# Experts in a fixed loop of 16 with four kinds of work, in place of a computed list of items

## The chip, the cores and the metric

The kernel runs on one core of one Trainium2 chip. The metric is device time in microseconds (us) of one execution; lower is better. A core has a matrix engine (TensorE, PE), a vector engine (VectorE, DVE), an activation engine (ScalarE, ACT), GpSimd (POOL) and SyncE (SP), which here only issues transfers. Each engine runs a program of its own and meets the others through semaphores.

## The reference, cut to what matters

Two layers, each a hybrid attention block and a mixture of experts, on 256 tokens of 1024 numbers, all in fp32. What the change touches is the second half of a layer:

```python
def grouped_moe(h, w_router, b_router, w_gate, w_up, w_down):
    probs = jax.nn.softmax(xt @ w_router + b_router)      # 256 tokens x 16 experts
    # 4 groups of 4 experts: the best group, then the best 2 experts inside it
    experts, gates = ...                                  # 512 (token, expert) pairs in all
    for each expert e, for the tokens that chose it:
        a = silu(x @ w_gate[e]) * (x @ w_up[e])           # 1024 x 1024 each
        out += gate * (a @ w_down[e])                     # 1024 x 1024
h = layer_norm(ALPHA * h + out)
```

Every expert's three matrices (4 MB each, 12.6 MB together) are read from HBM once in a layer, 16 experts, two layers.

## The kernel before, in words

**Staging of the weights.** `ring` is an SBUF buffer of 16 slots of 1 MB. Slots 0 to 3 (EVEN) and 12 to 15 (ODD) take the gate matrices of even and odd experts, 4 to 7 (UP) the up matrix, 8 to 11 (DOWN) the down matrix. SP issues the transfers in a fixed order (`load_matrix`, L335 to L344), two slots at a time, each after the semaphores `ring_free` of its slots. TensorE adds to `ring_free` when it has used a slot. So the weights run at most about an expert and a third ahead of TensorE.

**The list of items.** After the router, DVE counts the tokens of each expert (`count`, at most 256) and makes a list of at most 19 items (L1271 to L1305). An expert with more than 128 tokens has two items, each other expert one. For each item the list holds the expert's number (`expert_i`), a kind (`kind_i`) and whether it is the expert's last item (`last_i`); `n_i` is the number of items, and `start_i` the items of the layers before, from which every engine computes the values that it waits for. The kind is 0 (tiny, up to 32 tokens), 1 (narrow, up to 64), 2 or 3 (wide, the first or second 128 tokens).

**The loop over the items.** PE, ACT and DVE each run a loop over `n` items with a branch for each kind. In the PE's program (L856 to L890): read `expert_i`, `kind_i`, `odd_i` (and `last_i` where the item isn't tiny) from SBUF into registers (`value_load`), wait for `xg_ready` (the gathered tokens), then branch. For tiny items gate and up products run side by side (`tiny_gate_up`, L566); for narrow ones gate, then up (`narrow_gate`, `narrow_item`, L554); for wide ones likewise (`wide_gate`, `wide_item`, L670), and the wide code stands there twice: once for an expert's last item, which frees the ring's slots, once for one that is not. Then each item gathers the tokens of the next (L541), turns the activations, multiplies by the down matrix, and scatters into `acc` (L622, L729). ACT computes silu (L1008, L1014, L1020), DVE the product with up (L1324, L1333, L1342) and the 0/1 matrices that pick tokens (`place_tokens`, `place_gates`).

In the profiled execution each layer has 16 items, none of them a second half. With t for tiny, n for narrow and w for wide, in their order:

```
layer 0:  t n n n n n t t t t t n t t t t
layer 1:  w w t w t t n t t t t t t t t t
```

Of the kernel before, what the change touches and what calls it, by code (L numbers as in the profile page):

```python
# [52 lines left out]
MOST = NEXP + (2 * SEQ - 1) // (P + 1)  # L53
ITEMS = MOST + 1
# [23 lines left out]
C_L16 = C_LO + 8 * 16  # L78
C_ODD = C_L16 + NEXP * NEXP
# [3 lines left out]
def constants():  # L83
# [31 lines left out]
    t[:, C_L16:C_L16 + 256] = (e[None] <= e[:, None]).astype(np.float32).ravel()  # L115
# [44 lines left out]
def build(nc, x, w_in, w_out, w_gate, w_up, w_down, small, router, ln, consts, out):  # L160
    with ExitStack() as ctx:
# [42 lines left out]
        rank_tab = sb("rank_tab", [P, TB, NEXP])  # L204
        gate_tab = sb("gate_tab", [P, TB, NEXP])
        nsub = sb("nsub", [P, 2, NEXP])
        wide_shift = sb("wide_shift", [P, 1])
        wide = sb("wide", [P, NEXP + 1])
        kind_step = sb("kind_step", [P, 2, NEXP])
        itab = sb("itab", [P, 4, ITEMS])  # L210
        startf = sb("startf", [P, DEPTH + 1])

        start_i = sb("start_i", [P, DEPTH + 1], I32)
        n_i = sb("n_i", [P, DEPTH], I32)
        expert_i = sb("expert_i", [P, DEPTH * ITEMS], I32)
        kind_i = sb("kind_i", [P, DEPTH * ITEMS], I32)
        odd_i = sb("odd_i", [P, NEXP], I32)
        last_i = sb("last_i", [P, DEPTH * ITEMS], I32)
# [80 lines left out]
        plan_ready = sem("plan_ready")  # L299
        dve_step = sem("dve_step")  # L300

        place_ready, gathered, xg_ready = sem("place_ready"), sem("gathered"), sem("xg_ready")
# [97 lines left out]
        def _(pe):  # L400
# [135 lines left out]
            def gather(ks, release=None):  # L536


                for k in ks:
# [6 lines left out]
                    if k % 4 == 3:  # L546
                        mm.then_inc(gathered, 1)
# [10 lines left out]
            def turn_gates():  # L558
# [3 lines left out]
                mm.then_inc(placeT_done, 1)  # L562
# [6 lines left out]
            def tiny_gate_up(first, gate_full, full):  # L569


                for i in range(4):
# [13 lines left out]
                    else:  # L586
                        gate.then_inc(gate_done, 1)
                        up0.then_inc(ring_free[first + 3], 1)
                        up1.then_inc(up_done, 1)

            def tiny_item(full, g, turn):

                pe.wait_ge(place_ready, turn + 1)
                gather(range(3), ring_free[UP + 3])
                pe.wait_ge(act_ready, g + 1)
                turn_gates()
                for b in range(4):
                    mm = nc.tensor.transpose(lo[:, 1, b * W:(b + 1) * W], act[0:W, b * P:(b + 1) * P], ident[0:W, 0:W])
                mm.then_inc(act_turned, 1)
                gather(range(3, 4))  # L600
                pe.wait_ge(act_t_ready, g + 1)
                for s in range(4):
# [8 lines left out]
                    mm.then_inc(down_done if s == 3 else ring_free[DOWN + s], 1)  # L611
                pe.wait_ge(placeT_ready, g + 1)
                gather(range(4, KB), ring_free[DOWN + 3])
                scatter_halves(g)

            def scatter_halves(g):

                pe.wait_ge(y_ready, g + 1)
# [5 lines left out]
                mm.then_inc(scattered, 1)  # L624

            def narrow_gate(first, gate_full, full):

                for i in range(4):
# [5 lines left out]
                    mm.then_inc(gate_done if i == 3 else ring_free[first + i], 1)  # L634
# [3 lines left out]
            def narrow_item(full, g, turn):  # L638

                for i in range(4):  # L640
# [4 lines left out]
                    mm.then_inc(up_done if i == 3 else ring_free[UP + i], 1)  # L645
                pe.wait_ge(place_ready, turn + 1)
                gather(range(3), ring_free[UP + 3])
                pe.wait_ge(act_ready, g + 1)
                for b in range(4):
                    mm = nc.tensor.transpose(lo[:, 1, b * P:(b + 1) * P], act[:, b * P:(b + 1) * P], ident)  # L650
                mm.then_inc(act_turned, 1)
                turn_gates()
                gather(range(3, 4))
                pe.wait_ge(act_t_ready, g + 1)
# [19 lines left out]
            def wide_gate(last, first, gate_full, full):  # L674

                for i in range(4):
# [5 lines left out]
                    if i == 3:  # L682
                        mm.then_inc(gate_done, 1)
                    elif last:
                        mm.then_inc(ring_free[first + i], 1)
# [689 lines left out]
```

## Time and profile before

| what | value |
|---|---|
| median of 3 runs | 1367.46 us (1367.44 to 1370.69) |
| the profiled execution's own time | 1370.7 us |
| its span, first to last instruction | 1369.0 us |
| mean granted TensorE clock | 0.908 |
| busy: PE, DVE, ACT | 1122.7, 312.4, 182.1 us |
| DMA | 444.83 MB, mean 325 GB/s |
| chain that ended last | PE 61%, DMA 29%, issue 6%, DVE 3% |

How to read it: the span is cut into 40 slices of 34.2 us, and a row of GB/s gives what DMA moved in each. Where this stands at about 429, DMA is full. "issue" in the chain is time in which an engine waited for nothing that the profile shows. The engines' own control instructions (register, branch, value loads) are not counted as busy, but the view of a source line lists them with their durations, under names such as PEldq and DVEq.

### The profile page before, as it was taken

The numbers are of one execution on the slowest core, as the hardware profiler recorded it, in microseconds if no ns is written. First come the engines' busy times: TensorE is split into PE (matmuls) and PEld (weight loads), VectorE is DVE, ScalarE is ACT, GpSimd is POOL, SyncE is SP. The second block draws the span as 40 slices with busy tenths as digits, with TensorE's granted clock in tenths as the row PEclk, the third lists the DMA queues.
The fourth block names the chain that finished last, engine by engine and source line by source line (L and its number), as shares of the span: only waits on it lengthen the run. The fifth ranks groups of instructions, "written<-read, shape, count | busy, mean of one in ns | idle before, by whom it ended". The sixth has DMA issues, their size and how long they took to land.

```text
span 1369.0 us, 17057 instructions
## 1 busy us (share of the span) xinstructions
PE 1122.7 (82%) x6068; PEld 571.9 (42%) x6069; DVE 312.4 (23%) x791; ACT 182.1 (13%) x373; POOL 4.6 (0%) x12
## 2 busy tenths in 40 slices
PE   7999877799977768679799975999998876577775
PEld 5776443344433233224577644445443332222232
DVE  0443531111111111112254443001111111111113
ACT  2233210001000100001223320100000100000100
POOL 0000000000000000000000000000000000000000
PEclk9999878899988899789899986999999998778888
DMA  9814319899999999999931430656989999999994
GB/s 367 360 62 164 143 44 426 350 419 428 429 428 428 429 428 429 429 428 423 419 135 62 185 143 13 246 199 264 383 326 374 429 429 428 428 428 428 428 429 204
DMA packets 34712, 444.83 MB, mean 325 GB/s; under 512 B 4080, under 2 KB 4336, under 8 KB 5872
## 3 DMA queue, kind: packets, MB, share of 16 engines
q1 hardware_dynamic: 33520, 440.08, 77.6%
q0 software_dynamic: 1152, 4.19, 0.8%
q8 instruction: 27, 0.44, 0.1%
q14 instruction: 13, 0.11, 0.0%
HBM read 443.22 MB, written 1.05 MB: 325 GB/s over the span
## 4 chain that ended last, share of the span: by engine, by line
PE 61%; DMA 29%; issue 6%; DVE 3%; SPq 1%; ACT 0%; DVEq 0%; ACTq 0%
DMA ring<-in_w_up_dram 23%; PE lo L566 13%; PE lo L670 9%; PE lo L554 9%; PE acc L453 8%; DMA ring<-in_w_down_dram 6%; PE acc L431 5%; PE lo L541 3%; PE acc L529 3%; PE acc L622 1%; PE lo L836 1%; PE acc L505 1%; PE lo L493 1%; PE acc L729 1%; PE lo L529 1%
## 5 line engine op out<-in xcount | busy, mean ns | idle before, releaser
L566 PE MATMUL lo<-ring,work 128*32 128x512 f32 x2112 | 276.0, 671 | 150.7 <-DMA ring<-in_w_up_dram 131.4
L566 PEld LDWEIGHTS lo<-ring,work 128*32 128x32 f32 x2112 | 68.2, 121 | 339.0 <-issue 164.0
L554 PE MATMUL lo<-ring,work 128*64 128x512 f32 x672 | 153.0, 611 | 26.4 <-issue 23.5
L541 PEld LDWEIGHTS lo<-work,h 128*128 128x128 f32 x1088 | 130.2, 193 | 53.8 <-issue 49.7
L541 PE MATMUL lo<-work,h 128*128 128x128 f32 x1088 | 146.6, 285 | 2.5 <-DVE work L1266 2.5
L670 PE MATMUL lo<-ring,work 128*128 128x512 f32 x288 | 126.8, 601 | 15.8 <-issue 15.8
L453 PE MATMUL acc<-actT,ring 128*128 128x256 f32 x512 | 119.2, 388 | 0.0
L453 PEld LDWEIGHTS acc<-actT,ring 128*128 128x128 f32 x512 | 98.6, 195 | 14.7 <-issue 1.6
L554 PEld LDWEIGHTS lo<-ring,work 128*64 128x64 f32 x672 | 48.3, 140 | 125.9 <-issue 116.6
L670 PEld LDWEIGHTS lo<-ring,work 128*128 128x128 f32 x288 | 55.2, 193 | 84.7 <-issue 84.7
L1324 DVE TENSOR_TENSOR work<-lo,work 64x512 f32<-64x512 f32 x22 | 15.0, 682 | 291.8 <-ACT work L1008 291.8
L1008 ACT ACTIVATE work<-lo 64x512 f32<-64x512 f32 x22 | 13.1, 593 | 492.2 <-PE lo L566 492.2
L431 PE MATMUL acc<-ring,actT 128*128 128x512 f32 x128 | 63.3, 640 | 4.0 <-ACT actT L909 4.0
L622 PE MATMUL acc<-work 64*128 64x512 f32 x232 | 57.6, 615 | 0.0
L1145 DVE COPY work<-lo 128x512 f32<-128x512 f32 x64 | 44.3, 692 | 56.9 <-PE lo L541 56.8
L529 PE MATMUL acc<-ring,work 128*128 128x512 f32 x104 | 48.9, 602 | 0.0
L431 PEld LDWEIGHTS acc<-ring,actT 128*128 128x128 f32 x128 | 25.1, 204 | 32.1 <-issue 30.7
L406 PE MATMUL lo<-cst,h 128*128 128x128 f32 x64 | 12.8, 365 | 25.9 <-DVE h L1053 18.2
L1329 DVE COPY work<-lo 128x512 f32<-128x512 f32 x22 | 15.2, 692 | 78.9 <-PE lo L566 78.9
L1333 DVE TENSOR_TENSOR work<-lo,work 128x512 f32<-128x512 f32 x7 | 4.8, 692 | 115.3 <-PE lo L554 115.3
L1138 DVE TENSOR_SCALAR work<-cst,rank_tab,gate_tab 128x128 f32 x64 | 19.3, 344 | 51.9 <-issue 51.9
L1008 ACT ACT_TABLE_LOAD x22 | 28.2, 1283 | 18.6 <-issue 18.5
(183 smaller groups left out, 691.8 us busy)
## 6 DMA issues: line engine op xcount, KB each, us to landing
ring<-in_w_gate_dram SPq DMA_DIRECT2D x64, 2048.0 KB, 12.9
ring<-in_w_up_dram SPq DMA_DIRECT2D x64, 2048.0 KB, 18.7
ring<-in_w_down_dram SPq DMA_DIRECT2D x64, 2048.0 KB, 24.1
ring<-in_w_in_dram SPq DMA_DIRECT2D x24, 1024.0 KB, 25.0
ring<-in_w_out_dram SPq DMA_DIRECT2D x8, 1024.0 KB, 29.5
ln_gb<-in_ln_dram POOLq DMA_DIRECT2D x8, 512.0 KB, 7.0
cst<-in_consts_dram SPq DMA_DIRECT2D x1, 1544.0 KB, 17.9
h<-in_x_dram SPq DMA_DIRECT2D x1, 1024.0 KB, 5.2
```

Of the source, the lines that this page charges most:

```text
L431: mm = nc.tensor.matmul(acc[:, 3 if u else 1, :], actT[:, k, t * P:(t + 1) * P], ring[:, s, (k % 4) * CH:(k % 4 + 1) * CH], start=(k == 0) ...
L453: mm = nc.tensor.matmul(acc[:, 1, i * SEQ:(i + 1) * SEQ], ring[:, s, at:at + P], actT[:, k, :], start=(k == 0 and i == 0), stop=(k == KB - ...
L529: mm = nc.tensor.matmul(banks[half], oT[:, k, t * P:(t + 1) * P], wout[:, k, half * 512:(half + 1) * 512], start=(k == first), stop=(k == ...
L541: mm = nc.tensor.matmul(lo[:, 2 + k // 4, (k % 4) * P:(k % 4 + 1) * P], h[:, t, k * P:(k + 1) * P], place_t[:, t], start=(k % 4 == 0 and t ...
L554: mm = nc.tensor.matmul(lo[half * W:(half + 1) * W, bank, :], lhsT, ring[:, s, at:at + 512], start=start, stop=stop, skip_group_check=True)
L566: return nc.tensor.matmul(lo[at * T:(at + 1) * T, bank, :], lhsT, ring[:, s, col:col + 512], start=start, stop=stop, skip_group_check=True)
L622: mm = nc.tensor.matmul(acc[:, 2 * t + half, :], place_gt[r, t * P:(t + 1) * P], y[r, 0:512], start=False, stop=True, skip_group_check=True)
L670: mm = nc.tensor.matmul(lo[:, bank + half, :], lhsT, ring[:, s, at:at + 512], start=start, stop=stop, skip_group_check=True)
L1008: nc.scalar.activation(silu[0:W, 0:512], lo[W:P, 0, :], ACT.Silu).then_inc(silu_done, 1)
L1138: nc.vector.tensor_scalar(place_tg[:, t], places[:, bass.ds(kind * P, P)], rank_tab[:, t, bass.ds(expert, 1)], gate_tab[:, t, bass.ds(expe ...
L1145: op = nc.vector.tensor_copy(xg[:, 4 * half:4 * half + 4, :], lo[:, 2 + half, :].rearrange("p (k s) -> p k s", k=4))
L1329: nc.vector.tensor_copy(y[:, 0:512], lo[:, 0, :]).then_inc(y_ready, 1)
```

## The change

The list goes. All three engines run a loop of exactly 16 passes, one for each expert, so that the expert's number is the loop's counter and need not be read. `kind` is now 0 to 3, where 3 is an expert with more than 128 tokens, whose two halves are worked in one pass by code of their own. Each expert adds 2 (`WHOLE`) to the item semaphores whatever its kind (each half of kind 3 adds 1), so the values waited for follow from the loops' counters. `place_i` (kind, at most 2) says which numbering of tokens the expert uses.

```diff
-MOST = NEXP + (2 * SEQ - 1) // (P + 1)
-ITEMS = MOST + 1
+WHOLE = 2
+DONE = WHOLE * NEXP
+TURNED = DONE + WHOLE
...
         @block.tensor
...
-                turn0 = pe.snap(start + l + 1)
-                pe.wait_ge(place_ready, turn0)
-                gather(range(KB))
-                pe.wait_ge(plan_ready, l + 2)
-                n = pe.value_load(n_i[0:1, bass.ds(l, 1)], min_val=NEXP, max_val=MOST)
-                with pe.Fori(0, n) as j:
-                    g = pe.snap(start + j)
-                    turn = pe.snap(turn0 + j)
-                    expert = pe.value_load(expert_i[0:1, bass.ds(l * ITEMS + j, 1)], min_val=0, max_val=NEXP - 1)
-                    kind = pe.value_load(kind_i[0:1, bass.ds(l * ITEMS + j, 1)], min_val=0, max_val=3)
-                    odd = pe.value_load(odd_i[0:1, bass.ds(expert, 1)], min_val=0, max_val=1)
...
-                    pe.wait_ge(xg_ready, turn)
-                    with pe.If(kind < 1):
+                pe.wait_ge(place_ready, l * TURNED + WHOLE)
+                gather(range(KB), WHOLE)
+                pe.wait_ge(kinds_ready, l + 2)
+                pe.sem_inc(passed, 1)
+                with pe.Fori(0, NEXP) as j:
+                    done = pe.snap(l * DONE + j * WHOLE + WHOLE)
+                    turn = pe.snap(l * TURNED + j * WHOLE + WHOLE)
+                    kind_j = pe.value_load(kind_i[0:1, bass.ds(l * (NEXP + 1) + j, 1)], min_val=0, max_val=3)
+                    odd = pe.value_load(odd_i[0:1, bass.ds(j, 1)], min_val=0, max_val=1)
...
+                    with pe.If(kind_j < 1):
...
-                        last = pe.value_load(last_i[0:1, bass.ds(l * ITEMS + j, 1)], min_val=0, max_val=1)
...
-                            with pe.If(last > 0):
+                            with pe.If(kind_j < 3):
                                 with pe.If(odd < 1):
-                                    wide_gate(True, EVEN, even_full, full)
+                                    wide_gate(EVEN, even_full, full, turn, True, WHOLE)
                                 with pe.Else():
-                                    wide_gate(True, ODD, odd_full, full)
-                                wide_item(True, full, g, turn)
+                                    wide_gate(ODD, odd_full, full, turn, True, WHOLE)
+                                wide_item(full, done, turn + WHOLE, True, WHOLE)
                             with pe.Else():
-                                with pe.If(odd < 1):
-                                    wide_gate(False, EVEN, even_full, full)
-                                with pe.Else():
-                                    wide_gate(False, ODD, odd_full, full)
-                                wide_item(False, full, g, turn)
+                                for last in (False, True):
+                                    with pe.If(odd < 1):
+                                        wide_gate(EVEN, even_full, full, turn + last, last, 1)
+                                    with pe.Else():
+                                        wide_gate(ODD, odd_full, full, turn + last, last, 1)
+                                    wide_item(full, done - (not last), turn + 1 + last, last, 1)
...
         @block.scalar
-                a.wait_ge(gathered, a.snap(2 * start + 2 * l + 2))
                 for b in range(2):
+                    a.wait_ge(gathered[b], l * TURNED + WHOLE)
                     op = nc.scalar.copy(xg[:, 4 * b:4 * b + 4, :], lo[:, 2 + b, :].rearrange("p (k s) -> p k s", k=4))
-                op.then_inc(xg_ready, 1)
+                op.then_inc(xg_ready, WHOLE)
...
         @block.vector
-                step(nc.vector.tensor_scalar(wide[:, 0:NEXP], count, T + 0.5, None, ALU.is_gt))
...
+                step(nc.vector.tensor_scalar(kind[:], count, T + 0.5, None, ALU.is_gt))
+                step(nc.vector.scalar_tensor_tensor(out=kind[:], in0=count, scalar=W + 0.5, in1=kind[:],
+                                                    op0=ALU.is_gt, op1=ALU.add))
+                step(nc.vector.scalar_tensor_tensor(out=kind[:], in0=count, scalar=P + 0.5, in1=kind[:],
+                                                    op0=ALU.is_gt, op1=ALU.add))
+                own = l * (NEXP + 1)
                 nc.vector.tensor_copy(odd_i[:], cst[:, C_ODD:C_END])
+                nc.vector.tensor_scalar(place_i[:, bass.ds(own, NEXP)], kind[:], 2.0, None, ALU.min)
+                nc.vector.tensor_copy(kind_i[:, bass.ds(own, NEXP)], kind[:]).then_inc(kinds_ready, 1)
```

In DVE's loop `place_tokens` for the next expert moves behind the branch on the kind, into each branch, and three values are read in a pass (`kind_i`, `place_i` of this and of the next expert) where there were four. At the start of each layer every engine no longer reads `start_i`.

At the head of the PE's loop the order of the program is, before (TENSOR_LOAD is the read of a value into a register, ISA and REGISTER_ALU are register instructions):

```order
L856 UNCONDITIONAL_BRANCH
L856 ISA
L859 TENSOR_LOAD expert_i
L859 ISA x2
L860 REGISTER_ALU
L860 TENSOR_LOAD kind_i
L860 ISA x2
L861 ISA
L861 TENSOR_LOAD odd_i
L861 ISA x2
L865 REGISTER_ALU
L866 COMPARE_AND_BRANCH [waits xg_ready]
```

and in the change:

```order
L846 UNCONDITIONAL_BRANCH [waits kinds_ready]
L846 ISA
L849 TENSOR_LOAD kind_i
L849 ISA x2
L850 ISA
L850 TENSOR_LOAD odd_i
L850 ISA x2
L854 COMPARE_AND_BRANCH
L855 COMPARE_AND_BRANCH
```

The read of the expert's number is gone, and the wait for `xg_ready` stands behind the branches. Further on, the read of `last_i`, which narrow and wide items had, is gone as well.

In ACT's branch for a tiny expert the program before has the load of the activation table ahead of the wait for the gate product:

```order
L1007 ISA
L1008 ACT_TABLE_LOAD
L1008 ACTIVATE work<-lo 64x512 [waits gate_done]
L1010 COPY work<-lo 128x256 [waits act_turned]
L1006 UNCONDITIONAL_BRANCH
```

and the change has it behind that wait:

```order
L1003 ISA
L1004 ACT_TABLE_LOAD [waits gate_done]
L1004 ACTIVATE work<-lo 64x512
L1006 COPY work<-lo 128x256 [waits act_turned]
L1002 UNCONDITIONAL_BRANCH
```

An instruction that adds 2 to a semaphore no longer carries a wait of its own; the wait is an instruction ahead of it, and the table load now stands between the two. The narrow branch moves in the same way, the wide one doesn't.

What DVE does between the count and the loop, in the change:

```order
L1276 TENSOR_SCALAR kind<-lo 128x16
L1031 REGISTER_ALU
L1277 SCALAR_TENSOR_TENSOR kind<-lo,kind 128x16 [waits dve_step]
L1031 REGISTER_ALU
L1279 SCALAR_TENSOR_TENSOR kind<-lo,kind 128x16 [waits dve_step]
L1031 REGISTER_ALU
L1282 CAST odd_i<-cst 128x16 [waits dve_step]
L1283 ISA
L1283 TENSOR_SCALAR place_i<-kind 128x16
L1284 REGISTER_ALU
L1284 COPY kind_i<-kind 128x16
```

Six operations stand where the program before has 21, L1271 to L1305.

The size of the PE's program, counted from its order of instructions, each fp32 product as four (two passes, each a weight load and a matmul) and each transpose as two:

| part of the PE's program | before | change |
|---|---|---|
| a layer up to the experts' loop | 1610 | 1602 |
| the loop's head, the first branch with it | 15 | 10 |
| tiny: even gate, odd gate, the rest | 132, 131, 160 | 133, 132, 160 |
| narrow: branch, even gate, odd gate, the rest | 6, 75, 74, 217 | 2, 76, 75, 217 |
| wide: branch, even gate, odd gate, the rest | 2, 75, 74, 225 | 2, 76, 75, 225 |
| a further piece of code for wide: before, an item that isn't its expert's last; in the change, both halves of kind 3 | 375 | 748 |
| the loop's end | 4 | 4 |

The last piece but one is not entered in an execution on these inputs, before or in the change; every pass jumps over it to the loop's end, and from there back to the head.

## Rows read from the trace of the kernel before

**Rows 1.** The page: GB/s in 40 slices of 34.2 us.

```profile
GB/s 367 360 62 164 143 44 426 350 419 428 429 428 428 429 428 429 429 428 423 419 135 62 185 143 13 246 199 264 383 326 374 429 429 428 428 428 428 428 429 204
```

**Rows 2.** Stretches: us, busy (x instructions) by engine, PE clock, DMA share, GB/s.

```profile
195.00:216.00 21.00, 20.15 (x142) 8.40 (x142) 3.73 (x8) 2.25 (x3) 0.00 (x0) 0.84 0.60 238
291.00:320.00 29.00, 27.35 (x144) 11.78 (x142) 4.28 (x9) 2.46 (x3) 0.00 (x0) 1.00 1.01 425
```

**Rows 3.** Chain in order of time, layer 0: start us, us, what.

```profile
191.80 3.99 issue
195.79 10.03 PE lo L566 x62
216.35 8.01 issue
291.75 1.64 issue
```

**Rows 4.** The same chain in layer 1.

```profile
839.29 10.52 issue
849.81 29.66 PE lo L670 x64
903.77 1.46 issue
905.23 27.74 PE lo L670 x64
958.65 7.01 PE lo L566 x62
```

**Rows 5.** Timeline ahead of layer 0's loop: start us, us, engine, line, operation.

```profile
185.89 0.17 DVE L1271 TENSOR_SCALAR wide<-lo 128x16 f32<-128x16 f32 x1
186.03 3.84 PE L541 MATMUL lo<-work,h 128*128 128x128 f32 x32 [1.24 <-DVE work L1266]
189.90 1.07 ACT L998 COPY work<-lo 128x512 f32<-128x512 f32 x2 [10.80 <-PE lo L541]
191.64 0.15 DVE L1305 CAST start_i<-startf  x1
```

**Rows 6.** PE's control instructions by line: durations ns min/median/max, first and last start us.

```profile
L866 PEldq COMPARE_BRANCH  x1: 6441/6441/6441, 213.3 to 213.3; - x1
L874 PEldq COMPARE_BRANCH  x1: 6197/6197/6197, 251.2 to 251.2; - x1
L866 PEldq COMPARE_BRANCH  x1: 3533/3533/3533, 842.7 to 842.7; - x1
L874 PEldq COMPARE_BRANCH  x1: 2267/2267/2267, 847.0 to 847.0; - x1
L873 PEldq ALU_OP  x1: 44/44/44, 292.1 to 292.1; - x1
L873 PEldq SEQ_ASSERT  x1: 18/18/18, 292.8 to 292.8; - x1
```

**Rows 7.** DMA queues: whole span; 262 to 645 us (nothing else); 840 to 852; 677.7 to 784.9 us.

```profile
q8 instruction: 27, 0.44, 0.1%
...
q1 hardware_dynamic: 11127, 161.06, 99.2%
...
q8 instruction: 3, 0.05, 1.6%
...
q8 instruction: 3, 0.05, 0.2%
```

**Rows 8.** A stretch of layer 1's attention, columns as in rows 2.

```profile
677.65:784.96 107.31, 107.31 (x504) 75.58 (x503) 47.33 (x137) 31.81 (x94) 0.00 (x0) 1.00 0.38 145
```

**Rows 9.** The page, costliest groups: ACT's table loads for tiny items.

```profile
L1008 ACT ACT_TABLE_LOAD x22 | 28.2, 1283 | 18.6 <-issue 18.5
```

**Rows 10.** SP's issues of gate loads, the first in layer 0, one in layer 1.

```profile
202.68 3.71 SPq L343 DMA_DIRECT2D ring<-in_w_gate_dram  x2
...
1033.77 3.70 SPq L343 DMA_DIRECT2D ring<-in_w_gate_dram  x2
```

More of the change, by code:

```diff
@@ L534, in mix, with gather @@
                 return mm
-            def gather(ks, release=None):
+            def gather(ks, n, release=None):
                 for k in ks:
@@ L567, in quarter, with tiny_gate_up @@
                                         start=start, stop=stop, skip_group_check=True)
-            def tiny_gate_up(first, gate_full, full):
+            def tiny_gate_up(first, gate_full, full, turn):
+                pe.wait_ge(xg_ready, turn)
                 for i in range(4):
@@ L672, in wide_product, with wide_gate @@
                 return mm
-            def wide_gate(last, first, gate_full, full):
+            def wide_gate(first, gate_full, full, turn, last, n):
+                pe.wait_ge(xg_ready, turn)
                 for i in range(4):
@@ L689, in wide_gate, with wide_item @@
                     mm.then_inc(ring_free[first + 3], 1)
-            def wide_item(last, full, g, turn):
+            def wide_item(full, done, next_turn, last, n):
                 for i in range(4):
@@ L720, in wide_item @@
                     if s == 3:
-                        mm.then_inc(down_done, 1)
+                        mm.then_inc(down_done, n)
                     elif last:
                         mm.then_inc(ring_free[DOWN + s], 1)
-                pe.wait_ge(placeT_ready, g + 1)
-                gather(range(4, KB), ring_free[DOWN + 3] if last else None)
-                pe.wait_ge(y_ready, g + 1)
+                pe.wait_ge(placeT_ready, done)
+                gather(range(4, KB), n, ring_free[DOWN + 3] if last else None)
+                pe.wait_ge(y_ready, done)
                 for t in range(TB):
@@ L1001, in _ @@
+                a.wait_ge(kinds_ready, l + 2)
                 a.sem_inc(passed, 1)
[L1002 to L1025 removed]
@@ new lines, in wide_half @@
+                def wide_half(done, n):
+                    a.wait_ge(gate_done, done)
+                    for half in range(2):
+                        op = nc.scalar.activation(silu[:, half * 512:(half + 1) * 512], lo[:, half, :], ACT.Silu)
+                    op.then_inc(silu_done, n)
+                    a.wait_ge(act_turned, done)
+                    for half in range(2):
+                        op = nc.scalar.copy(act_t[:, half * 512:(half + 1) * 512], lo[:, half, :])
+                    op.then_inc(act_t_ready, n)
@@ new lines, in _ @@
+                with a.Fori(0, NEXP) as j:
+                    done = a.snap(l * DONE + j * WHOLE + WHOLE)
+                    kind_j = a.value_load(kind_i[0:1, bass.ds(l * (NEXP + 1) + j, 1)], min_val=0, max_val=3)
+                    with a.If(kind_j < 1):
+                        a.wait_ge(gate_done, done)
+                        nc.scalar.activation(silu[0:W, 0:512], lo[W:P, 0, :], ACT.Silu).then_inc(silu_done, WHOLE)
+                        a.wait_ge(act_turned, done)
+                        nc.scalar.copy(act_t[:, 0:4 * W], lo[:, 1, 0:4 * W]).then_inc(act_t_ready, WHOLE)
+                    with a.Else():
+                        with a.If(kind_j < 2):
+                            a.wait_ge(gate_done, done)
+                            nc.scalar.activation(silu[:, 0:512], lo[:, 0, :], ACT.Silu).then_inc(silu_done, WHOLE)
+                            a.wait_ge(act_turned, done)
+                            nc.scalar.copy(act_t[:, 0:512], lo[:, 1, :]).then_inc(act_t_ready, WHOLE)
+                        with a.Else():
+                            with a.If(kind_j < 3):
+                                wide_half(done, WHOLE)
+                            with a.Else():
+                                wide_half(done - 1, 1)
+                                wide_half(done, 1)
```

327 lines of the change are left out of this document (137 added, 190 removed).

## The prediction

> **What bounds the kernel now.** I read the page's 40 slices first [rows 1]. In layer 0's experts (from about 205 us) DMA moves 426 to 429 GB/s, the most it reaches anywhere, but for two slices, 350 and 419: there it lacks 79 and 10 of 429 over 34.2 us each, 7.1 us of idleness. In layer 1 six slices of the experts (from 856 us) are at 199 to 383, then DMA is full to the end. So work saved on TensorE counts where a layer's loop starts and until DMA is full; in layer 0 that is before its third item, in layer 1 up to the fifth (w w t w t). Behind these points a faster PE only waits longer for weights. SP's rows tell why a start moves everything behind it: the first expert load of layer 0 is issued at 202.68, when the first item has freed two slots, and in layer 1 one at 1033.77, just behind the start of the fifth item [rows 10].
>
> The chain in order of time shows holes without a visible cause: 3.99 us ahead of layer 0's loop, 8.01 us before its second item, but 1.64 before the fourth [rows 3]; 10.52 us ahead of layer 1's loop and 1.46 between its two wide items [rows 4]. The PE's control instructions explain them. Reading one value takes from 292.1 to 292.8, about 0.75 us with what follows. And four branches, which elsewhere take 0.1 to 0.3 us, last 6.44, 6.20, 3.53 and 2.27 us [rows 6].
>
> **What these branches wait for.** Queue q8 fetches 27 pieces of 16 KB of program, and three of them fall into the 12 us of the last two long branches [rows 7]. Between two such fetches PE passes some 256 instructions: three lie strictly inside 677.7 to 784.9 us and one at either edge, so four intervals for 504 + 503 records and some 20 control instructions [rows 8]. From 262 to 645 us there is no fetch at all, though 14 items are worked and all jump back [rows 7]. So blocks stay near the engine, and some number of them fits. I laid the parts' sizes (table in the section on the change) end to end in blocks of 256 and followed the items. The account that fits is this: there are 8 places in a ring; entering a block fetches the next one ahead into the next place; a jump to an absent block waits for it. It yields 27 fetches, none in 262 to 645 us, and long branches where the rows have them: at the end of items 0 and 1 of layer 0 (jump over the unused wide code to the loop's end) and at two jumps in layer 1's first item. Counted from the layer's start as block 0, the loop begins in block 6 and ends in block 12. With the block fetched ahead, 6 to 13 are 8 blocks: they just fit.
>
> The Trainium skill, Runtime: NRT & Kernel Launch, Instruction fetch mechanics, has blocks of 16 KiB and 128 KiB for PE, which the count above agrees with. The same section says that a taken branch to a block outside two pages fetches anew; 383 us of items without a fetch speak against that, and the trace decides.
>
> **The change, part by part.** Costs are against the profiled execution, 1370.7 us.
>
> *The shorter preparation.* DVE starts counting kinds at 185.89 and ends the list at 191.64 + 0.15 [rows 5]. Of 21 operations 6 stay; at about 0.2 us each they end at 187.1, 4.7 us earlier. In layer 0 PE then reads two values (1.5 us, and 0.7 for branches) until 189.4, which lies under its gather (186.03 + 3.84 = 189.87). ACT's second copy, half of 1.07, follows: 190.5. PE's first product starts at 190.6 instead of 195.79: -5.2.
>
> *The clock.* After the hole of 3.99 us the clock granted is 0.84 in the first item, but 1.00 after one of 1.64 [rows 2]. PE's idle time now is 0.7 us, so I take the full clock: 62 matmuls in 7.01 [rows 4] instead of 10.03 [rows 3]: -3.0.
>
> *The table load.* It takes 1.283 us [rows 9] and now follows the gate product. A narrow item hides it (its up product follows, some 7 us), a tiny one doesn't: PE waits for the activation at once. +1.3 in layer 0's first item and in layer 1's third; in the other 20 tiny items the wait for weights covers it.
>
> *Reads.* The expert's number and, in narrow and wide items, `last_i` are gone: 0.75 each. Before layer 0's items 1 and 2: -1.5 each. Both keep their long branch, since the loop's end is still absent there (item 0), then displaced by a block fetched ahead (item 1). From item 3 on DMA is full and the 1.5 us, which lie in the hole of 1.64, are worth nothing.
>
> Layer 0: -5.2 - 3.0 + 1.3 - 1.5 - 1.5 = -9.9. The weights follow: the first load is issued some 8 us earlier, and the idle 7.1 us of DMA, which end with item 2's first release, shrink by 1.7.
>
> *Layer 1's start.* Preparation -4.7, one read -0.7: -5.4. The other read is swallowed by the same wait for a block.
>
> *The longer program.* The unused code goes from 375 to 748 instructions, the loop from 6.1 to 7.5 blocks: its end moves from block 12 to block 14 (13 if fewer than 46 instructions stand ahead of the program). Layer 0 enters no wide code and its blocks still fit. A wide item in layer 1 uses 6, 8, 9, 10, 11 and the end, and fetches 12 and 15 ahead: with 7 for tiny ones that is nine or ten blocks in 8 places. Each fetch throws out what is needed next. Following the items:
> - end of item 0 (w): the loop's end is absent; fetching ahead behind it throws out block 6, so the jump back waits; then block 8, then 9 still on its way;
> - end of item 1 (w) and of item 3 (w): the loop's end and block 6 each;
> - item 2 (t) fits; from item 4 on only tiny and narrow items, which fit.
>
> Seven long branches and one shorter. Prices: 3.53 with DMA idle, 6.44 and 6.20 with DMA full, 2.27 for a block on its way [rows 6]. DMA is half loaded here (199 to 264 GB/s), and drains while PE stands: I take 5.0 for each and 3.0 for the shorter, 38.0. None of it is covered, as PE's hole before these items is 1.46 us or nothing: PE ends just when its branches do. Off go the reads, 1.5 + 0.75 + 0.75 here and 1.5 before item 3. The stalls cool the clock: the first wide item took 29.66 after a long hole and the second 27.74 without [rows 4], +1.9; for the tiny items after items 1 and 3, 10.03 against 7.01, +3.0 each. With the table load:
> 38.0 - 4.5 + 7.9 + 1.3 = +42.7.
> DMA does not absorb it: it waits for slots that these items free (1033.77).
>
> **Sum:** -9.9 - 5.4 + 42.7 = +27.4, so 1398 us for a profiled execution, and with the same distance from the median (1370.7 lies 3.2 above 1367.46) **1395 us**.
>
> **Bounds.** All seven at 3.53 and the shorter at 2.27: 27.0, 11 less. All at 6.44, the shorter too: 51.5, 13.5 more. So 1384 to 1408. If DMA hides half of the last pair or the clock stays up, up to 12 us more go: 1372.
>
> **Rivals.**
> 1. *The blocks still fit* (other side). Should more than 8 be kept, or the sizes be off: with fewer than 28 instructions ahead of the program the wide item ends inside block 10, block 12 is never fetched and only one extra branch waits. Then -9.9 - 5.4 - 1.5 - 1.5 + 1.3 = -17.0: 1350; with one wait of 5 to 6 and a cool clock, 1358. For it: the edge is near. Against it: the account meets all 27 fetches, and block 12 was fetched before this change during the wide item, by the same rule. 0.12. It decides from the ninth block on.
> 2. *Everything hidden*: gains lost under DMA and few stalls, within 0.3% of 1367. Against it: a loop's start shifts the first weights 1:1. 0.03.
> 3. *Worse displacement*: tiny and narrow items miss too, also where DMA is not full; above 1410. Against it: these use 6 to 10 and the end, which fit. 0.03.
> 4. *Jumps never reuse blocks* (the page's two pages): the end's jump would wait in every item, before and after, and the change would only save: 1350. Rows 7 exclude it; within rival 1's chance.
>
> **How the numbers follow.** The displacement has 0.82; its bounds reach from 1372 to 1410, which holds close to 8 in 10 of all. A measurement tells this kernel's times apart at about 0.3%, 4 us. Faster 0.12, same 0.03, slower 0.85.
>
> **What the changed profile would show.** q8 near 51 pieces instead of 27, the additional ones between 900 and 1060 us; long branches at the end of layer 1's items 0, 1 and 3 and at the head behind them; layer 0's first PE product near 190.6, at full clock; PE waiting some 1.3 us for the activation in a tiny item; a hole of nearly nothing before layer 0's fourth item. I am wrong if q8 stays near 27, if the new stalls cost under 3 us each, or if DMA is full in layer 1 in spite of them.

## The result

The change makes the kernel slower. Its median is 1401.78 us (4 runs, 1397.42 to 1405.49) beside 1367.45 for the kernel before on the same chip: a ratio of 1.0245, 95% interval 1.0211 to 1.0280, so +2.1 to +2.8%. The prediction was 1395, range 1372 to 1410. The profiled execution took 1402.45 us, its span is 1400.7, 31.7 longer than before. Of all executions reported here, one of e8_pad_long stands apart (1905.51 us at a granted clock of 0.554, its three others 1401.05 to 1404.45), which no run explains; its ratio leaves it out.

The page of the changed kernel answers to [rows 1], [rows 7] and [rows 9]. The slices are 35.0 us now; then the table loads, and PE's transposes behind them.

```profile
GB/s 367 339 61 181 150 166 428 373 431 428 428 429 429 429 428 429 429 429 416 192 53 173 130 83 240 124 240 175 386 282 244 431 427 428 429 430 427 428 428 194
...
q8 instruction: 51, 0.84, 0.3%
...
L1004 ACT ACT_TABLE_LOAD x22 | 28.2, 1283 | 541.0 <-PE lo L558 541.0
...
L553 PE MATMUL lo<-cst,work 128*128 128x128 f32 x64 | 13.5, 292 | 28.8 <-DVE work L1301 28.8
```

Layer 0 is as full of DMA as it was. In layer 1 the slices before the full stretch now stand at 240, 124, 240, 175, 386, 282, 244. q8 counts 51 pieces of program, for 27 before.

The chain of the changed kernel in order of time (start us, us, what; x62 counts instructions) answers to [rows 3] and [rows 4]. Layer 0:

```profile
190.93 7.08 PE lo L558 x62
...
198.09 1.28 ACT L1004
...
209.86 6.28 issue
...
643.04 1.15 issue
```

The first product starts at 190.93 for 195.79 and takes 7.08 for 10.03, the table load stands on the chain, and the hole before the second item is 6.28 for 8.01. The layer's last hole is at 643.04; before the change it stood at 653.42:

```profile
653.42 1.15 issue
```

So layer 0 gained 10.4 us. Layer 1 in the changed kernel:

```profile
829.06 6.36 issue
835.42 30.14 PE lo L663 x64
...
888.99 16.19 issue
905.18 29.40 PE lo L663 x64
...
958.00 9.84 issue
967.84 9.83 PE lo L558 x62
...
977.74 1.28 ACT L1004
...
990.27 1.55 PE lo L663 x3
991.82 3.15 issue
994.96 29.20 PE lo L663 x61
...
1047.58 10.37 issue
1057.94 9.20 PE lo L558 x63
...
1068.08 14.24 DMA ring<-in_w_up_dram
```

The loop still starts 14.4 us earlier than before (835.42 for 849.81). Then come three long holes of 16.19, 9.84 and 10.37 us, where there had been 1.46, none and none. A fourth of 3.15 stands inside a gate product. By the second item the lead is gone (905.18 for 905.23). The same chain before the change went on so, behind [rows 4]:

```profile
978.11 27.74 PE lo L670 x64
...
1029.88 7.06 PE lo L566 x63
...
1037.88 13.36 DMA ring<-in_w_up_dram
```

The wait for DMA ended at 1037.88 + 13.36 = 1051.24 before and ends at 1082.32 now, 31.1 later. From there DMA is full in both, and the 31.1 reach the end as 31.7.

The first two holes are these branches of PE (control instructions by line, duration in ns, start us). The third long one is two more, 6600 ns at L868 and 4982 at L846.

```profile
L868 PEldq COMPARE_BRANCH  x1: 6183/6183/6183, 885.2 to 885.2; - x1
...
L846 PEldq COMPARE_BRANCH  x1: 4560/4560/4560, 891.5 to 891.5; - x1
...
L854 PEldq COMPARE_BRANCH  x1: 3414/3414/3414, 897.8 to 897.8; - x1
...
L861 PEldq COMPARE_BRANCH  x1: 3147/3147/3147, 901.3 to 901.3; - x1
...
L868 PEldq COMPARE_BRANCH  x1: 6443/6443/6443, 954.2 to 954.2; - x1
...
L846 PEldq COMPARE_BRANCH  x1: 4620/4620/4620, 960.9 to 960.9; - x1
```

They stand where the prediction put them: at the end of items 0, 1 and 3 (L868, the jump over kind 3's code) and at the head behind them (L846), and two more in the first of these pairs. Most of the 24 additional pieces of q8 lie in the stretch 883 to 1062 us, which holds 22 now and held 2 before:

```profile
q8 instruction: 22, 0.36, 1.0%
```

What DMA moved during three of these branches goes with their lengths (windows 885.2 to 891.4, 891.5 to 896, 897.8 to 901.2 us of the same kernel):

```profile
DMA packets 133, 1.97 MB, mean 317 GB/s; under 512 B 13, under 2 KB 13, under 8 KB 13
...
q8 instruction: 1, 0.02, 0.9%
...
DMA packets 5, 0.05 MB, mean 11 GB/s; under 512 B 2, under 2 KB 2, under 8 KB 2
...
q8 instruction: 2, 0.03, 4.5%
...
DMA packets 1, 0.02 MB, mean 5 GB/s; under 512 B 0, under 2 KB 0, under 8 KB 0
...
q8 instruction: 1, 0.02, 1.9%
```

With weights moving at 317 GB/s the branch takes 6.18 us; with DMA nearly idle it takes 3.41, and 4.56 where two pieces fall into the wait. The other pairs repeat it: 6.44 at 315 GB/s and 6.60 at 298, then 4.62 at 11 and 4.98 at 10.

### The profile page after: what moved, and what is told of

Its sections match the earlier page's. It is cut to its first block, busy times and chain, and to the rows that moved or that the text cites. A ratio compares the mean times of both kernels' runs of the same rounds, so it can differ in the third digit from the quotient of the medians.

```text
span 1400.7 us, 16826 instructions
## 1 busy us (share of the span) xinstructions
PE 1134.6 (81%) x6068; PEld 577.0 (41%) x6069; DVE 301.2 (22%) x760; ACT 182.4 (13%) x373; POOL 4.6 (0%) x12
## 4 chain that ended last, share of the span: by engine, by line
PE 61%; DMA 27%; issue 6%; DVE 3%; ACT 1%; SPq 1%; DVEq 0%; ACTq 0%
DMA ring<-in_w_up_dram 27%; PE lo L558 15%; PE lo L663 9%; PE acc L445 8%; PE lo L546 8%; PE acc L423 4%; PE lo L533 3%; PE acc L521 3%; PE acc L614 1%; PE lo L827 1%; PE acc L497 1%; PE lo L485 1%; PE acc L723 1%; PE lo L521 1%; SPq L335 1%
## 5 line engine op out<-in xcount | busy, mean ns | idle before, releaser
L558 PE MATMUL lo<-ring,work 128*32 128x512 f32 x2112 | 281.3, 688 | 142.4 <-DMA ring<-in_w_up_dram 121.0
L558 PEld LDWEIGHTS lo<-ring,work 128*32 128x32 f32 x2112 | 71.9, 124 | 333.5 <-issue 193.0
L546 PE MATMUL lo<-ring,work 128*64 128x512 f32 x672 | 152.3, 608 | 18.8 <-issue 12.8
L663 PE MATMUL lo<-ring,work 128*128 128x512 f32 x288 | 131.9, 619 | 27.1 <-issue 27.1
L445 PE MATMUL acc<-actT,ring 128*128 128x256 f32 x512 | 122.6, 396 | 0.0
L445 PEld LDWEIGHTS acc<-actT,ring 128*128 128x128 f32 x512 | 100.7, 199 | 15.9 <-issue 1.6
L553 PE MATMUL lo<-cst,work 128*128 128x128 f32 x64 | 13.5, 292 | 28.8 <-DVE work L1301 28.8
```

The costliest lines, as they stand in the source:

```text
L445: mm = nc.tensor.matmul(acc[:, 1, i * SEQ:(i + 1) * SEQ], ring[:, s, at:at + P], actT[:, k, :], start=(k == 0 and i == 0), stop=(k == KB - ...
L546: mm = nc.tensor.matmul(lo[half * W:(half + 1) * W, bank, :], lhsT, ring[:, s, at:at + 512], start=start, stop=stop, skip_group_check=True)
L558: return nc.tensor.matmul(lo[at * T:(at + 1) * T, bank, :], lhsT, ring[:, s, col:col + 512], start=start, stop=stop, skip_group_check=True)
L663: mm = nc.tensor.matmul(lo[:, bank + half, :], lhsT, ring[:, s, at:at + 512], start=start, stop=stop, skip_group_check=True)
```

## The experiments

Theory A is the prediction's: the never entered code makes a wide item of layer 1 touch more program blocks than stay near PE, and each return waits. Rival B: the semaphore adds of 2, with waits ahead of them and the table load behind, cost the time. "The account" is the prediction's way of following the items through blocks of 256 instructions with 8 places.

| kernel | median us | ratio to before (95%) | span us | q8 |
|---|---|---|---|---|
| e2_before_longer | 1421.60 | 1.0388 (1.0371 to 1.0406) | 1421.5 | 51 |
| e1_no_kind3 | 1350.37 | 0.9870 (0.9854 to 0.9887) | 1350.0 | 26 |
| e7_pad_short | 1350.60 | 0.9867 (0.9849 to 0.9885) | 1350.3 | 27 |
| e8_pad_long | 1402.85 | 1.0251 (1.0225 to 1.0278) | 1399.3 | 51 |
| e13_pad_ahead | 1360.96 | 0.9931 (0.9909 to 0.9954) | 1359.1 | 30 |
| e4_compact | 1361.00 | 0.9948 (0.9930 to 0.9967) | 1359.0 | 27 |
| e10_compact_late_adds | 1355.28 | 0.9894 (0.9865 to 0.9922) | 1353.2 | 27 |
| e3_table_first | 1399.38 | 1.0231 (1.0211 to 1.0250) | 1397.3 | 51 |
| e9_late_kinds | 1353.14 | 0.9883 (0.9864 to 0.9902) | 1353.6 | 26 |
| e12_later_kinds | 1365.14 | 0.9957 (0.9938 to 0.9977) | 1363.9 | 26 |
| e11_more_reads | 1361.31 | 0.9943 (0.9917 to 0.9970) | 1360.5 | 26 |

e13, e11 and e12 ran on another chip, where the kernel before had 1370.32, for 1367.65 to 1367.85 beside the others, so their ratios are compared, not their medians. The inputs have no expert with more than 128 tokens, so the code for kind 3 never runs in any of these kernels.

**e2_before_longer.** The kernel before, longer by code that nothing enters.

```diff
-                                with pe.If(odd < 1):
-                                    wide_gate(False, EVEN, even_full, full)
-                                with pe.Else():
-                                    wide_gate(False, ODD, odd_full, full)
-                                wide_item(False, full, g, turn)
+                                for _ in range(2):
+                                    with pe.If(odd < 1):
+                                        wide_gate(False, EVEN, even_full, full)
+                                    with pe.Else():
+                                        wide_gate(False, ODD, odd_full, full)
+                                    wide_item(False, full, g, turn)
```

> The kernel before, with its never entered wide code written twice (375 more PE instructions that no execution reaches). Nothing that runs is changed. Theory A: the loop ends in block 14 instead of 12, q8 counts 51 pieces, and the time rises by the long branches (about 40 us) and by the clock and the wait on a block fetched ahead (about 8 us): 1413 (1403 to 1422). Layer 0 keeps its time. Rival B (length of code never entered is free): 1367, q8 27.

Measured: 1421.60, q8 51, at the upper end of what was expected. Nothing that runs was changed and the kernel lost 54 us, so unused code alone can cost this much, and the rival that its length is free falls. Whether the adds, waits and table loads of B have a part in the change is left to e1_no_kind3. The holes of its chain in layer 1:

```profile
901.84 20.27 issue
...
976.24 11.08 issue
...
1007.08 7.18 issue
...
1068.38 10.62 issue
```

The third lies inside no pair that I had counted: it is the jump to the odd gate of item 3 (a branch of 5.31 us). By the account it lands in a block that is only just being fetched; q8 moves one piece during it.

**e1_no_kind3.** The other way round: the change without the long unused piece.

```diff
-                            with pe.If(kind_j < 3):
-                                with pe.If(odd < 1):
...
-                            with pe.Else():
-                                for last in (False, True):
...
+                            with pe.If(odd < 1):
+                                wide_gate(EVEN, even_full, full, turn, True, WHOLE)
+                            with pe.Else():
+                                wide_gate(ODD, odd_full, full, turn, True, WHOLE)
+                            wide_item(full, done, turn + WHOLE, True, WHOLE)
```

> The change with the PE's code for kind 3 left out (an expert with more than 128 tokens would be computed wrongly; there is none in these inputs). The PE's loop is 748 instructions shorter and ends in block 11 or 12 instead of 14; all else stays, the adds of 2, the waits ahead of them and the table load too. Theory A (program blocks displaced): the 40 us of long branches in layer 1 and what the clock and item 3 lost go, the earlier starts of both layers stay (10.4 us in layer 0, 4.0 more in layer 1), so 1367 - 14 - 3 + 1 = about 1351 (1345 to 1358), q8 27 pieces or fewer. Rival B (the adds of 2, the waits that stand alone and the table load cost the time): about 1395 to 1402, whatever q8 counts.

Measured: 1350.37, q8 26. Its chain has the layer's start of the change (835.72) and then no hole between the wide items:

```profile
835.72 30.10 PE lo L663 x64
...
889.25 27.48 PE lo L663 x64
...
940.15 7.01 PE lo L558 x62
...
959.32 27.74 PE lo L663 x64
...
1010.48 7.06 PE lo L558 x63
```

q8 fetches nothing between 883 and 1062 us. Everything of B is still in this kernel, so B is not the cause. This is the reference for what the unused code costs: 1400.7 - 1350.0 = 50.7 us of span. It also shows that all the rest of the change together is a gain of 1.1 to 1.5%.

**e7_pad_short and e8_pad_long.** Is it an edge, or a price in proportion? Both are the change with kind 3's code replaced by transposes that nothing enters, 215 or 255 of them.

```diff
                             with pe.Else():
-                                for last in (False, True):
...
+                                for _ in range(215):     # 255 in e8_pad_long
+                                    nc.tensor.transpose(lo[:, 3, 0:P], place_tg[:, 0], ident)
```

> The change, but its kind 3 branch in the PE's program holds only 215 transposes (430 instructions, never entered) in place of the 748, and kind 3 would be computed wrongly. By the account the loop's end lies in block 12 (at 12.8) and q8 counts 27 pieces. Theory A: as e1_no_kind3 but for a branch of 0.2 us in three wide items, 1351 (1347 to 1355). Rival B2 (each block of program more costs in proportion, no edge): between e1_no_kind3 (1350) and the change (1402) by its 430 of 748 instructions, 1380.

> As e7_pad_short, with 40 transposes more in the branch that is never entered (510 instructions): by the account the loop's end moves to 13.1, the ninth block is touched, and q8 counts 51 pieces. Theory A: the long branches and the cold clock of the change are back in full, 1400 (1393 to 1406), 45 to 52 us for 80 instructions that no execution reaches. Rival B2 (in proportion): 6 us more than e7_pad_short at the most.

Measured: 1350.60 and 1402.85, on one chip. The page's line of the first, then of the second:

```profile
q8 instruction: 27, 0.44, 0.1%
```

```profile
q8 instruction: 51, 0.84, 0.3%
```

430 instructions cost nothing (ratio 0.9867, and 0.9870 for e1_no_kind3), 80 more cost 52 us (1.0251), and the change's 748 cost no more than 510. The account had put the loop's end at 12.8 and 13.1 blocks. It is an edge, and rival B2 falls.

**e13_pad_ahead.** Does the whole program's length decide, or what the loop touches? This is e1_no_kind3 with the same 255 transposes ahead of the loop.

```diff
+                first = pe.value_load(kind_i[0:1, bass.ds(l * (NEXP + 1), 1)], min_val=0, max_val=4)
+                with pe.If(first > 3):
+                    for _ in range(255):
+                        nc.tensor.transpose(lo[:, 3, 0:P], place_tg[:, 0], ident)
                 with pe.Fori(0, NEXP) as j:
```

> e1_no_kind3 with 255 transposes that are never entered (511 instructions) placed ahead of the experts' loop, behind one more read of a value and a branch in each layer. PE's program is as long as in e8_pad_long and its loop ends at the same place (13.1), but the loop itself spans only blocks 8 to 13. Theory A (what counts is how many blocks the items' loop touches in turn): q8 30 pieces, in each layer one more long branch of about 3.5 us at the jump over the new code and 0.9 us of read and branch: 1359 (1354 to 1364). Rival G (the length of the whole program, or the distance of the end from the layer's start, decides): as e8_pad_long, about 1402 and q8 near 50.

Measured: ratio 0.9931, 8 us above e1_no_kind3, q8 30, and the two long branches at the new code:

```profile
L847 PEldq COMPARE_BRANCH  x2: 3764/3819/3874, 186.9 to 832.8; - x2
```

The program ends where e8's does and costs 44 us less by ratio. So it is the set of blocks that successive items touch. Rival G falls. The 8 us are these two branches, the added read, and a cooler clock: PE now stands for 5.43 us ahead of layer 0's first product, which takes 9.08 us for 7.07.

**e4_compact and e10_compact_late_adds.** Versions that keep kind 3 and a short loop. e4, cut:

```diff
                             with pe.If(kind_j < 3):
+                                pe.wait_ge(xg_ready, turn)
+                                for s in (gate_done, up_done, act_turned, placeT_done, *gathered, down_done, scattered):
+                                    pe.sem_inc(s, 1)
+                            with pe.Else():
...
+                                wide_item(full, done - 1, turn + 1, False, 1)
+                            here = pe.snap(turn + kind_j - 2)
+                            with pe.If(odd < 1):
+                                wide_gate(EVEN, even_full, full, here, True, 1)
...
+                            wide_item(full, done, turn + WHOLE, True, 1)
```

> The change with kind 3 worked in two pieces: its first half by code of its own, its second half by the same code as kind 2 (which adds 1 by hand to the PE's eight semaphores ahead of it and 1 at each end). It computes what the change computes, for any counts, and the PE's loop is as long as before the change (ends in block 12). Theory A: q8 27 pieces, about 1351 (1345 to 1358), perhaps 1 us more for the hand-made adds. Rival B: 1395 or more. Rival D (more than one block lies between the edge and here, so that e1 gets its gain and this does not): q8 near 51 and about 1400.

Measured: 1361.00, q8 27: the gain is there, but 3 us outside the expectation. Its trace shows three costs beside e1_no_kind3: the jump over the first half's code waits once (3.54 us, in layer 1's first item); the second product of layer 1's item 2 takes 5.32 us for 3.64; and the eight adds stand ahead of each wide item, one each 0.15 us:

```profile
L871 PEldq EVENT_SEMAPHORE  x8: 51/51/51, 963.7 to 964.8; - x8
```

e10 moves six of the adds into `wide_item`, ahead of `pe.wait_ge(act_ready, done)`, where PE waits for DVE anyway, and has e3's table load:

```diff
-                                for s in (gate_done, up_done, act_turned, placeT_done, *gathered, down_done, scattered):
+                                for s in (gate_done, up_done):
...
+                    with pe.If(kind_j < 3):
+                        for s in (act_turned, placeT_done, *gathered, down_done, scattered):
+                            pe.sem_inc(s, 1)
                 pe.wait_ge(act_ready, done)
```

> e4_compact with only two of its eight hand-made adds ahead of the gate product, the other six just before PE's wait for DVE's product in the wide item, and the table load ahead of its wait. It computes what the change computes for any counts. In e4_compact the eight adds took 1.2 us (0.15 each) ahead of every wide item and are behind none. Theory A: 0.7 us in each of three wide items and 1 to 2.5 us of the table load less than e4_compact's 1361: 1357 (1355 to 1360), q8 27. Rival (the adds were covered): 1359 to 1361.

Measured: 1355.28, ratio 0.9894 (0.9865 to 0.9922), which is faster than both kernels. It is written to compute the same for any counts, but its code for kind 3 did not run here. As it has both edits, what each gave is not shown apart.

**e3_table_first.** The change with the table load off the chain.

```diff
+                        nc.scalar.activation(warm[:], ident[:, 0:1], ACT.Silu)
                         a.wait_ge(gate_done, done)
                         nc.scalar.activation(silu[0:W, 0:512], lo[W:P, 0, :], ACT.Silu).then_inc(silu_done, WHOLE)
```

> The change, with an activation of one column ahead of the wait for the gate product in ACT's tiny branch, so that the table load again lies before the wait. On the change's chain the table load stands in layer 0's first tiny item, in the last two tiny items of each layer and in layer 1's item 2: six times 1.28 us. Theory A: each of them is given back unless the next wait takes it, so 3 to 7.7 us less than the change, 1396 (1393 to 1400), q8 still 51. Rival C (the loads are covered by weights that come later anyway): 1402.

Measured: 1399.38 beside the change's 1401.78, 2.4 less where I had expected 3 to 7.7, and two ratios whose intervals overlap; its span is 3.4 shorter. At a layer's end nearly nothing came of it: its last hole in layer 0 is at 642.70 for 643.04, and its chain has a wait of 17.04 us for the down weights in place of the table loads. Rival C is not excluded, and the size of this term stays unclear between 0 and 3 us.

**e9_late_kinds and e12_later_kinds.** This tests the terms of the preparation and of the clock: e1_no_kind3, with 15 or 32 operations more on DVE.

```diff
+                for _ in range(15):     # 32 in e12_later_kinds
+                    step(nc.vector.tensor_copy(kind[:], kind[:]))
                 nc.vector.tensor_copy(odd_i[:], cst[:, C_ODD:C_END])
```

> e1_no_kind3 with 15 more operations of 16 columns on DVE ahead of the release of the kinds, as many as the change took out (each copies the kinds onto themselves). It tests the term of the preparation and that of the clock. Theory A: PE's first product in layer 0 starts 3.5 to 5 us later and takes about 10 us for 7.1, in layer 1 the loop starts 3.5 to 4.5 us later with the wide item as it was: 1350.4 + 8 + 4 = 1362 (1358 to 1365). Rival E (only the start moves, the clock does not care): 1358 to 1359. Rival F (both are made up for by DMA behind the start): 1350 to 1353.

> e9_late_kinds with 32 added operations instead of 15 (17 more, some 0.22 us each). In e9_late_kinds PE stood for 2.35 us ahead of layer 0's loop and its first 62 matmuls still took 7.08. Theory A (a hole of 4 us or more costs the clock): first product at about 196.5 and taking about 10 us, layer 0 ends 6 to 7 us later than e9_late_kinds, layer 1 another 3.7: 1363 (1360 to 1366). Rival E (only the start moves): 62 matmuls in 7.1, 1360 to 1361. Rival F (DMA makes it up): 1353 to 1356.

Measured: ratio 0.9883 and 0.9957, that is 2 and 12 us above e1_no_kind3. e9 missed what I expected (1358 to 1365): the start came only 1.75 us later and the clock held. PE's timeline ahead of the first product, for e1_no_kind3, e9, e12 and the kernel before (the bracket is PE's idle time ahead of it):

```profile
191.09 7.07 PE L558 MATMUL lo<-ring,work 128*32 128x512 f32 x64 [1.00 <-ACT work L976]
```

```profile
192.84 7.07 PE L558 MATMUL lo<-ring,work 128*32 128x512 f32 x64 [3.04 <-issue]
```

```profile
195.66 8.76 PE L558 MATMUL lo<-ring,work 128*32 128x512 f32 x64 [4.97 <-issue]
```

```profile
195.79 9.58 PE L566 MATMUL lo<-ring,work 128*32 128x512 f32 x60 [5.92 <-issue]
```

After 1.00 and 3.04 us of idleness the product takes 7.07, after 4.97 it takes 8.76, and the clock granted in the stretch 190 to 212 us is 1.00, 1.00 and 0.86. So both terms exist, but for smaller delays the start alone moves. In both kernels the delay reaches the layer's end: 3.0 us later in e9 for 1.75 at the start, 7.7 in e12 for 4.6 at the start and 3.4 of clock (1.7 in each of the first item's two products, where I had expected 3 in the first). Rival E, that only the start moves, falls for the longer delay, and rival F, that DMA makes it up, with it.

The idle time just ahead is not all that decides. In e8_pad_long the first product also follows 1.00 us of idleness and takes 7.07, but starts earlier, at 188.42. Then the item's second product takes 5.34 us, for 3.64 in e1_no_kind3:

```profile
199.81 5.34 PE L558 MATMUL lo<-ring,work 128*32 128x512 f32 x32
```

The clock granted in its stretch 200 to 204 us is 0.57, for 1.00 in e1_no_kind3. What tells the two apart is not shown.

**e11_more_reads.** The term of the reads: e1_no_kind3 with two more reads in each pass.

```diff
                     odd = pe.value_load(odd_i[0:1, bass.ds(j, 1)], min_val=0, max_val=1)
+                    pe.value_load(odd_i[0:1, bass.ds(j, 1)], min_val=0, max_val=1)
+                    pe.value_load(odd_i[0:1, bass.ds(j, 1)], min_val=0, max_val=1)
```

> e1_no_kind3 with two more reads of a value at the head of the PE's loop. It tests the term of the reads (0.75 us each) and where it counts. Theory A: 1.5 us each ahead of items 1 and 2 in layer 0 and up to 1.5 more at its start, nothing from item 3 on; in layer 1 1.3 to 1.5 ahead of each of the first five items: 3 + 7 = 10 us, 1360 (1356 to 1363). Rival H (the reads lie under PE's own queue of matmuls): 1350 to 1352.

Measured: ratio 0.9943, 10 us above e1_no_kind3, as expected in sum. But in layer 0 PE also stood ahead of the fourth to sixth items:

```profile
285.57 1.50 issue
...
314.71 1.39 issue
...
343.74 1.49 issue
```

The layer ended 5.3 us later (648.61 for 643.30), where I had 3 to 4.5. Rival H falls.

## Why the prediction was right

**The displacement** is shown from four sides: e2 makes the kernel before slow with code that never runs, e1 takes that code out of the change and the loss is gone, e7 and e8 find the edge between 12.8 and 13.1 blocks, e13 shows that the loop's own blocks count. q8 was 51 as the account had it. The account also gave the counts of e2, e7, e8, e4 and e13 (51, 27, 51, 27 and 30) ahead of their runs. Rivals 1 to 3 fall by the result, and rival 4 (jumps never reuse blocks) with them: in e1_no_kind3 q8 fetches nothing between 883 and 1062 us, though PE jumps over unused branches and back in each pass. What is argued only is the inside of the account, that 8 places form a ring and which one is overwritten; it fits every count, but no run sees a place.

**Layer 0**: predicted -9.9, measured -10.4. Start 190.93 (190.6), product 7.08 (7.01), hole of 6.28 for 8.01, table load 1.28. That the reads are worth nothing from the fourth item on is not so: at its start PE was 11.7 us ahead (281.70 for 293.39), its own missing hole of 1.64 included, and the next two items gained 1.4 each, so that the lead was 14.5 at the sixth (337.25 for 351.71). DMA took some 4 of it back by the layer's end. e11 shows the same holes. So it is in part luck that -10.4 meets -9.9.

**Layer 1's start**: predicted -5.4, measured 14.39 - 10.38 = -4.0. The term itself was right: from PE's gather ahead of the loop to the first product it is 16.29 us before (849.81 - 833.52) and 10.89 now (835.42 - 824.53), 5.4 less. The other 1.4 went in the layer's attention, whose matmuls the change leaves alone; why is not shown. The same code before layer 0's gather differs by 2.5 us between the profiles of the change and of e8_pad_long (186.09 and 183.58).

**Layer 1's items**: predicted +42.7, measured from the loop's start to the end of the wait for DMA 246.9 for 201.4, +45.5. Item by item, from start to start, against the kernel before:

| from | before us | change us | difference | predicted |
|---|---|---|---|---|
| item 0 (w) | 55.42 | 69.76 | +14.3 | +16.5 |
| item 1 (w) | 53.42 | 62.66 | +9.2 | +11.2 |
| item 2 (t) | 19.46 | 22.43 | +3.0 | +2.8 |
| item 3 (w) | 51.77 | 67.67 | +15.9 | +9.3 |
| item 4 (t) to the end of the wait | 21.36 | 24.38 | +3.0 | +3.0 |

The eight branches took 39.9 us (6.18, 4.56, 3.41, 3.15, 6.44, 4.62, 6.60, 4.98) where I had 38.0; the holes they leave are 36.4, because the first part of a branch at an item's end lies under PE's last matmuls (the one at 885.2 begins 3.8 us before its hole at 888.99). "None of it is covered" was wrong by that much, and it made item 0 cheaper than predicted. Item 1 was cheaper for another reason: from the end of its gate product to its end the kernel before had lost 2.3 us (25.68 for 23.42 now), a cost that the prediction did not know and that the change doesn't have.

**The term that was mis-sized is item 3**, +15.9 for +9.3. The prediction says that item 2 fits and then gives item 3 only its end and the head behind it. But, by the same account, item 2 fetches block 9 ahead, which displaces block 10; item 3 then fetches 10 ahead on entering 9 and reaches it three matmuls later. I priced only jumps to absent blocks and, once, a block on its way. It cost 3.15 us behind three matmuls (the one piece of q8 between 991 and 996 us), and the gate product then took 1.55 + 29.20 for 27.74, 3.0 more, on a clock granted at 0.90 (window 995 to 1025 us). e2 has the same step at 5.31 us.

The rest: the parts add up to +31.1 for the +27.4 predicted, and the span grew by 31.7. The median lies 34.3 above the one before, as the distance of 3.2 between profile and median that I had carried over was 0.7 here. So the mechanism was right and the sum 3.7 short, with some luck: items 0 and 1 came out 4.2 below their terms and item 3 6.6 above its own.

## What to carry to other kernels

Code that is never entered has a price when a loop jumps over it: count the program blocks that one turn of the loop touches, with the one fetched ahead, before adding a special case to a loop body of this length; here, by the account, the step from eight blocks to nine cost 52 us, and unused code below it nothing. The rare case can share the common code (e10_compact_late_adds) or stand outside the loop (unused code there cost 8 us in e13_pad_ahead; a rare case that works from there was not built). What PE saved at a loop's start moved everything behind it, until DMA was full.

## What the runs showed of the hardware

- The edge is sharp: 80 PE instructions (40 transposes) that no execution reaches, 1350.60 to 1402.85 us (ratios 0.9867 and 1.0251).
- PE waits not only at jumps. Running on into a block fetched ahead too late cost 3.15 us, with no branch in that place.
- A jump to an absent block took 3.4 us with DMA nearly idle (5 GB/s), 4.6 to 5.0 where two pieces fell into the wait (10 to 11 GB/s), and 6.2 to 6.6 where weights moved at 298 to 317 GB/s.
- TensorE's granted clock was 1.00 behind 3.04 us of idleness ahead of the first product and 0.86 behind 4.97 (190 to 212 us), in kernels that differ by 17 small operations on DVE. In e8_pad_long it fell to 0.57 (200 to 204 us) with no more idle time ahead of the product than e1_no_kind3 had.
- A semaphore add of its own took PE's sequencer 0.15 us (eight between 963.7 and 964.8 us in e4_compact), though its record shows 51 ns.
